# Up products of four FFNs from seven block products in place of eight, with the down part added chunk by chunk

## The chip, the cores and the metric

The kernel runs on one core of a Trainium2 chip. The metric is the device time of one execution in microseconds (us); the runs shown are of the same build.

## The reference

x has 512 tokens and 1024 features (D = 1024, F = 2816), all in float32. FFN 0 belongs to a first block with a recurrent mixer and a convolution; FFN 1 to 4 belong to a second block with a pooling mixer and an attention with shared keys and values:

```
FFN 0:       u = conv(rmsnorm(x) @ w_up); x = x + rmsnorm((silu(gate) * val) @ w_down)
FFN 1 to 4:  x = x + 0.5 * (silu(u @ wg) * (u @ wu)) @ wd      u = rmsnorm_2(x, gain)
order:       first mixer, FFN 0, FFN 1, pooling mixer, FFN 2, shared keys/values (kv),
             FFN 3, attention (dq, attn, w_o), FFN 4, final norm
```

## The kernel before

**Layout.** Activations lie feature-major: xT is 128 partitions by 8 k-tiles of 512 tokens. A norm isn't applied to x. Its gain goes into the operand (xghi, xglo), and its factor R (one value for each token) is multiplied onto the product.

**Exactness.** Each float32 product is made of three matmuls on rounded parts. ScalarE copies raw to whi (the rounded high part), VectorE subtracts to get wlo, and `three` accumulates wlo x xhi, whi x xlo and whi x xhi into one PSUM bank (L827, L828, L829).

**Units.** Weights come in units of 1024 x 256 (1 MB) through two slots. SP loads raw, ScalarE writes whi (L552), VectorE writes wlo (L1219); GpSimd takes some of these splits (L455). A unit of an up product has two output tiles of 128 features, each of 8 k-tiles x 3 matmuls of 512 columns. FFN 1 to 4 each have 11 pairs of a gate unit (slot 0) and a value unit (slot 1).

**Stages of an FFN.** `first_units` works through the first pair tile by tile as the operand arrives, a loop does the other ten pairs, and all 22 gated tiles are kept as ahi and alo. Then `project` makes the down product: two loop turns of two column blocks, each of k-splits 8, 8 and 6, with four PSUM banks (`ring`). Out of PSUM, VectorE adds 0.5 times the group to xT (L1423). It makes the next operand's low part (L1229) and ScalarE its high part (L572) and its square, which GpSimd sums (L470).

**Order.** Every engine has one queue in program order; what runs next to what is fixed by where each instruction stands and by semaphores. `sum_norm` is the matmul with ones that completes a norm. At FFN 1 the residual of FFN 0 is first completed by `add_normed` (L1436, L1442); at FFN 2 the pooling sums (L319, L1524, L1549) run on VectorE and GpSimd; FFN 3 follows the narrow kv product (`key_extras` adds two matmuls), FFN 4 the projection w_o.

## Time and profile before

| | |
|---|---|
| median of 3 runs | 2567.89 us (2566.75 to 2568.83) |
| profiled execution, first to last instruction | 2566.1 us |
| what lies around the span, median less span | 1.8 us |
| TensorE busy | 2471.6 us, 96% |
| VectorE busy | 1284.2 us, 50% |
| ScalarE busy | 797.1 us, 31% |
| GpSimd busy | 279.6 us, 11% |

The profile is of one execution, which has no device time of its own beside its span; so a difference in the span is carried over to the median. Engines: PE is TensorE's matmuls, PEld its weight loads, DVE VectorE, ACT ScalarE, POOL GpSimd, SP the engine that issues the loads. Line numbers are those of the kernel. A matmul's duration in the profile reaches over the start of the next, so that neighbouring starts give the rate.

### The profile page before, as it was taken

How to read it: one execution, taken by the hardware profiler on the slowest of the kernel's cores; microseconds unless marked ns; L12 is line 12 of the kernel's file. 1: busy time of each engine (PE TensorE's matmuls, PEld its weight loads, DVE VectorE, ACT ScalarE, POOL GpSimd, SP SyncE). 2: the span in 40 equal slices, each digit the busy share in tenths (PEclk: the TensorE clock that was granted, in tenths of full speed). 3: DMA queues.
4: the chain of work that ended last, by engine and by line, in shares of the span. 5: the costliest groups of instructions: out<-in, count | busy, mean ns of one | idle time of the engine just before them, and what ended most of it. 6: DMA issues, size and time to landing. Idle time of an engine off the chain costs nothing.

```text
span 2566.1 us, 28434 instructions
## 1 busy us (share of the span) xinstructions
PE 2471.6 (96%) x10762; PEld 1956.1 (76%) x10762; DVE 1284.2 (50%) x1429; ACT 797.1 (31%) x892; POOL 279.6 (11%) x128
## 2 busy tenths in 40 slices
PE   7999799999899999789999999999989999999998
PEld 5888677788688888568888778888856668788886
DVE  5687578762544433664443354443376743444423
ACT  4324443332332222232223232222233332222221
POOL 1211322211200000410000000000121201000000
PEclk9999999999999999899999999999999999999999
DMA  4221223322233222222322233322220113322321
GB/s 145 82 66 50 79 85 98 97 91 90 66 98 98 90 91 98 81 62 86 98 94 91 86 99 98 98 94 90 74 58 21 33 49 98 98 87 93 94 91 61
DMA packets 217220, 215.51 MB, mean 84 GB/s; under 512 B 10321, under 2 KB 214736, under 8 KB 217168
## 3 DMA queue, kind: packets, MB, share of 16 engines
q1 hardware_dynamic: 216624, 214.61, 26.4%
q8 instruction: 34, 0.56, 0.1%
q10 hardware_dynamic: 544, 0.20, 0.0%
q14 instruction: 18, 0.15, 0.0%
HBM read 212.70 MB, written 2.10 MB: 84 GB/s over the span
## 4 chain that ended last, share of the span: by engine, by line
PE 90%; DVE 7%; ACT 2%; issue 1%; DMA 0%; DVEq 0%; POOL 0%; ACTq 0%
PE bank L827 28%; PE bank L829 28%; PE bank L828 27%; PE bank L1192 1%; PE bank L1162 1%; DVE xglo L1229 1%; PE bank L1165 1%; PE bank L926 1%; DVE xT L1442 1%; DVE wlo L1219 1%; ACT xghi L572 1%; ACT whi L552 1%; DVE work L1463 0%; DVE PT L1699 0%; DVE Y L1436 0%
## 5 line engine op out<-in xcount | busy, mean ns | idle before, releaser
L827 PE MATMUL bank<-xghi,wlo 128*128 128x512 f32 x2064 | 827.3, 401 | 61.6 <-DVE xglo L1229 59.4
L828 PE MATMUL bank<-xglo,whi 128*128 128x512 f32 x2064 | 820.2, 397 | 0.0
L829 PE MATMUL bank<-xghi,whi 128*128 128x512 f32 x2064 | 819.9, 397 | 0.0
L1219 DVE TENSOR_TENSOR wlo<-raw,whi 128x2048 fp32r<-128x2048 f32 x185 | 426.6, 2306 | 583.2 <-ACT whi L552 583.1
L552 ACT ACTIVATE whi<-raw 128x2048 fp32r<-128x2048 f32 x210 | 400.1, 1905 | 536.0 <-PE bank L829 525.0
L827 PEld LDWEIGHTS bank<-xghi,wlo 128*128 128x128 f32 x2064 | 390.3, 189 | 169.2 <-DVE xglo L1229 56.4
L829 PEld LDWEIGHTS bank<-xghi,whi 128*128 128x128 f32 x2064 | 390.0, 189 | 96.0
L828 PEld LDWEIGHTS bank<-xglo,whi 128*128 128x128 f32 x2064 | 390.7, 189 | 95.1 <-issue 1.7
L827 PE MATMUL bank<-ahi,wlo 128*128 128x512 f32 x880 | 347.6, 395 | 0.0
L829 PE MATMUL bank<-ahi,whi 128*128 128x512 f32 x880 | 347.6, 395 | 0.0
L828 PE MATMUL bank<-alo,whi 128*128 128x512 f32 x880 | 347.6, 395 | 0.0
L722 ACT ACTIVATE ahi<-work 128x512 f32 (+1 forms) x110 | 68.8, 636 | 460.7 <-DVE work L1491 460.7
L827 PEld LDWEIGHTS bank<-ahi,wlo 128*128 128x128 f32 x880 | 164.9, 187 | 40.6 <-issue 0.2
L829 PEld LDWEIGHTS bank<-ahi,whi 128*128 128x128 f32 x880 | 164.9, 187 | 40.5
L828 PEld LDWEIGHTS bank<-alo,whi 128*128 128x128 f32 x880 | 164.9, 187 | 40.2
L1482 DVE TENSOR_TENSOR work<-bank,R 128x512 f32<-128x512 f32 x110 | 75.0, 690 | 208.6 <-PE bank L829 206.9
L710 ACT ACTIVATE work<-work 128x512 f32<-128x512 f32 x110 | 69.4, 632 | 300.2 <-DVE work L1471 276.9
L455 POOL TENSOR_TENSOR wlo<-raw,whi 128x2048 fp32r<-128x2048 f32 x25 | 121.3, 4850 | 352.8 <-ACT whi L552 352.8
L470 POOL TENSOR_TENSOR acc<-sq 128x512 f32<-128x512 f32 x11 | 16.1, 1465 | 1263.7 <-ACT sq L679 1230.8
L1471 DVE TENSOR_TENSOR work<-bank,R 128x512 f32<-128x512 f32 x110 | 74.3, 687 | 153.8 <-PE bank L829 148.7
L470 POOL TENSOR_TENSOR acc<-acc,sq 128x512 f32<-128x512 f32 x62 | 86.9, 1401 | 508.4 <-ACT sq L679 480.5
L1463 DVE SCALAR_TENSOR_TENSOR work<-work,cw 128x511 f32<-128x511 f32 x88 | 110.5, 1266 | 14.6 <-ACT work L703 4.5
(231 smaller groups left out, 1857.6 us busy)
## 6 DMA issues: line engine op xcount, KB each, us to landing
raw<-in_ffn_w_up_dram SPq DMA_DIRECT2D x22, 1024.0 KB, 5.1
raw<-in_ffn_pre_wg_dram SPq DMA_DIRECT2D x22, 1024.0 KB, 5.3
raw<-in_ffn_pre_wu_dram SPq DMA_DIRECT2D x22, 1024.0 KB, 5.4
raw<-in_ffn_post_wg_dram SPq DMA_DIRECT2D x22, 1024.0 KB, 5.3
raw<-in_ffn_post_wu_dram SPq DMA_DIRECT2D x22, 1024.0 KB, 5.3
raw<-in_ffn_pre_wd_dram SPq DMA_DIRECT2D x16, 1024.0 KB, 5.2
raw<-in_ffn_post_wd_dram SPq DMA_DIRECT2D x16, 1024.0 KB, 5.2
raw<-in_w_in_dram SPq DMA_DIRECT2D x14, 1024.0 KB, 5.0
```

Source lines behind the costliest of these rows:

```text
L455: nc.gpsimd.tensor_tensor(wlo[:, c], raw[:, c], whi[:, c].bitcast(F32), ALU.subtract).then_inc(wlo_ready[s], 2)
L470: nc.gpsimd.tensor_tensor(acc[:, :], a0, tile(sq, k % 2), ALU.add).then_inc(acc_added, 1)
L552: nc.scalar.activation(whi[:, s * UNIT:(s + 1) * UNIT], raw[:, s * UNIT:(s + 1) * UNIT], ACT.Copy).then_inc(whi_ready[s], 2)
L710: nc.scalar.activation(tile(Tt, f), tile(Tt, f), ACT.Silu).then_inc(silu_ready, 1)
L722: nc.scalar.activation(tile(ahi, i * 2 + f), tile(At, f), ACT.Copy).then_inc(ahi_ready, 1)
L827: nc.tensor.matmul(bank, wlo_, xhi, start=first, stop=False)
L828: nc.tensor.matmul(bank, whi_, xlo, start=False, stop=False)
L829: return nc.tensor.matmul(bank, whi_, xhi, start=False, stop=last)
L1219: nc.vector.tensor_tensor(wlo[:, c], raw[:, c], whi[:, c].bitcast(F32), ALU.subtract).then_inc(wlo_ready[s], 2)
L1463: nc.vector.scalar_tensor_tensor(dst[:, sh:T], u[:, 0:T - sh], tap_col(i, tap, half, f), dst[:, sh:T], ALU.mult, ALU.add).then_inc(signal, 1)
L1471: nc.vector.tensor_tensor(tile(Ut if conv else Tt, f), ring[f][:, :], R[:, :], ALU.mult).then_inc(evacuated, 1)
L1482: nc.vector.tensor_tensor(tile(Ut if conv else At, f), ring[2 + f][:, :], R[:, :], ALU.mult).then_inc(evacuated, 1)
```

## The change

FFN 1 to 4 only. The up product of a unit (1024 x 256 weights, 512 tokens) is treated as a 2 x 2 block product. The weights are split by k-tile parity and by output tile, the tokens into two halves, and the block product is formed by the Winograd form of Strassen's scheme: seven block products of 128 x 128 by 256 columns for each of four pairs of k-tiles. In full:

- **Weights.** GpSimd makes the four sums of weight blocks (`unit_sums`): three into `sums`, one written over a raw block. ScalarE and VectorE split raw (2048 wide, part 0) and the sums (1536 wide, part 1) into high and low parts (`fill_up`).
- **Tokens.** For each pair of k-tiles `halves_act` widens the tiles with their gain into At, `halves_vec` makes the three differences into Tt, and both write seven half-width operands, high and low (`Xhi`, `Xlo`).
- **Products.** `chain` runs one of the seven (m1 to m7) over four pairs of k-tiles, 12 matmuls of 256 columns. Some partial results are copied out of PSUM by ScalarE (`keep`) and added by VectorE at the end (`take_unit`).
- **First pair.** `first_pair` runs m1, m2 and m4 as token operands arrive; m5, m6, m3 and m7 follow for both units.
- **Chunks.** The 11 pairs go in chunks of 2, 3, 3 and 3. After each chunk, `down_chunk` multiplies its 4 or 6 tiles (`chi`, `clo`) by their rows of the down weights for all 8 output tiles in 8 banks, and `take_down` adds 0.5 times each to xT. The 22-tile ahi and alo aren't used there.
- **Around it.** FFN 0's result is in Y1 and Ut, loops of FFN 1 to 4 and of w_o are unrolled, two pooling and kv operands get their own low part, oThi and oTlo lie where Xhi and Xlo of two token pairs lie, and the interleaving at each FFN's start is rewritten.

```diff
+CHUNKS = [2, 3, 3, 3]
+PAIR0 = [0, 2, 5, 8]
+UNIT0 = [0, 8, 18, 28]
...
+            def ffn(m):
+                which, l = FFN_WEIGHTS[m]
+                gate, val = kp(A[f"ffn_{which}_wg_2"][l]), kp(A[f"ffn_{which}_wu_2"][l])
+                down = kp(A[f"ffn_{which}_wd_2"][l])
+                for c, pairs in enumerate(CHUNKS):
+                    kt = 2 * pairs
+                    for i in range(PAIR0[c], PAIR0[c] + pairs):
+                        load(up_no(m, i, 0), 0, [(slot(raw, 0), gate[:, :, i * UC:(i + 1) * UC])])
+                        load(up_no(m, i, 1), 1, [(slot(raw, 1), val[:, :, i * UC:(i + 1) * UC])])
+                    k0 = 2 * PAIR0[c]
+                    for b in range(4):
+                        load(down_no(m, c, b), b % 2, [(slot(raw, b % 2, kt),
+                                                        down[:, k0:k0 + kt, b * UC:(b + 1) * UC])])
...
+            def unit_sums(m, i, h):
+                n, base = up_no(m, i, h), adds_base(m, i)
+                u = slot(raw, h).rearrange("p (j d) c -> p j d c", d=2)
+                a11, a12 = u[:, :, 0, 0:P], u[:, :, 1, 0:P]
+                a21, a22 = u[:, :, 0, P:2 * P], u[:, :, 1, P:2 * P]
+                s1, s2, s4 = (sums[h][:, k * 512:(k + 1) * 512].rearrange("p (j c) -> p j c", c=P) for k in range(3))
+                pool.wait_ge(raw_ready[h], (n - h) * 8 + 16)
+                nc.gpsimd.tensor_tensor(s1, a21, a22, ALU.add).then_inc(adds_done[h], 1)
+                nc.gpsimd.tensor_tensor(a21, a11, a21, ALU.subtract).then_inc(adds_done[h], 1)
+                pool.wait_ge(adds_done[h], base + 1)
+                nc.gpsimd.tensor_tensor(s2, s1, a11, ALU.subtract).then_inc(adds_done[h], 1)
+                pool.wait_ge(adds_done[h], base + 3)
+                nc.gpsimd.tensor_tensor(s4, a12, s2, ALU.subtract).then_inc(adds_done[h], 1)
+            def ffn_sums(m, first):
+                for i in range(first, FT // 2):
+                    unit_sums(m, i, 0)
+                    unit_sums(m, i, 1)
...
-            sum_squares("post_ffn", last_splits("down0", len(DOWN)))
-            for name in ("pre0", "mix0"):
-                sum_squares(name)
-            pool.wait_ge(groups_done, GB["pool"])
+            sum_squares("post_ffn", [UB["down0"] + 7, None])
+            pool.wait_ge(groups_done, GB["down0"] + 8)
+            unit_sums(1, 0, 0)
+            unit_sums(1, 0, 1)
+            sum_squares("pre0")
+            ffn_sums(1, 1)
+            sum_squares("mix0")
...
+            def fill_up(m, i, h, part, signal, value):
+                n = up_no(m, i, h)
+                if part == 0:
+                    a.wait_ge(raw_ready[h], (n - h) * 8 + 16)
+                    a.wait_ge(adds_done[h], adds_base(m, i) + 2)
+                    a.wait_ge(signal, value)
+                    nc.scalar.activation(whi[:, h * UNIT:(h + 1) * UNIT], raw[:, h * UNIT:(h + 1) * UNIT],
+                                         ACT.Copy).then_inc(whi_ready[h], 2)
+                else:
+                    a.wait_ge(adds_done[h], adds_base(m, i) + 4)
+                    a.wait_ge(signal, value)
+                    nc.scalar.activation(sxhi[h][:, :], sums[h][:, :], ACT.Copy).then_inc(whi_ready[h], 2)
+            def fill_down(m, c, b):
+                n, s, w = down_no(m, c, b), b % 2, 2 * CHUNKS[c] * UC
+                a.wait_ge(raw_ready[s], (n - s) * 8 + 16)
+                a.wait_ge(m7_done, strassen_no(m, PAIR0[c] + CHUNKS[c] - 1, b // 2) + 1)
+                dst = sxhi[b // 2][:, 0:w] if s else whi[:, (b // 2) * UNIT:(b // 2) * UNIT + w]
+                nc.scalar.activation(dst, raw[:, s * UNIT:s * UNIT + w], ACT.Copy).then_inc(whi_ready[s], 4)
...
+            def halves_act(m, pos, signal=None, value=None):
+                j = PAIR_ORDER[m][pos]
+                hi, (gain, off) = Xhi[PAIR_SLOT[m][j]], FFN_GAIN[m]
+                n = 4 * (m - 1) + pos
+                a.wait_ge(halves_ready, n)
+                for d in range(2):
+                    nc.scalar.activation(tile(At, d), tile(xT, 2 * j + d), ACT.Copy,
+                                         scale=col(gain, 2 * j + d + off)).then_inc(wide_ready, 1)
+                if signal is not None:
+                    a.wait_ge(signal, value)
+                a.wait_ge(wide_ready, 2 * n + 2)
+                nc.scalar.activation(hi[:, 0:HT], At[:, 0:HT], ACT.Copy).then_inc(halves_hi, 1)
+                nc.scalar.activation(hi[:, HT:3 * HT], At[:, T:2 * T], ACT.Copy).then_inc(halves_hi, 1)
+                a.wait_ge(halves_added, 3 * n + 3)
+                nc.scalar.activation(hi[:, 3 * HT:7 * HT], Tt, ACT.Copy).then_inc(halves_hi, 1)
...
+                for c, pairs in enumerate(CHUNKS):
+                    for i in range(PAIR0[c], PAIR0[c] + pairs):
+                        for h in range(2):
+                            if i == 0:
+                                continue
+                            fill_next(m, i, h, 0)
+                            keep(m, i, h, "m1")
+                            fill_next(m, i, h, 1)
+                            keep(m, i, h, "m5")
+                            if h:
+                                gate_act(m, i)
+                            elif i > PAIR0[c]:
+                                pair_act(m, i - 1)
+                            keep(m, i, h, "u2")
+                            keep(m, i, h, "m4")
+                    fill_down(m, c, 2)
+                    pair_act(m, PAIR0[c] + pairs - 1)
+                    fill_down(m, c, 3)
+                    if c + 1 < len(CHUNKS):
+                        for part in range(2):
+                            fill_up(m, PAIR0[c + 1], 0, part, down_done, group_no(m, c, 4))
...
+            for part in range(2):
+                fill_up(1, 0, 0, part, groups_done, GB["down0"] + 8)
             root("post_ffn")
-            for k in range(DT):
-                xg_hi(resid_ready, DT + k + 1, xT, "ffn_pre_norm_2", k)
-                square("pre0", k, xT)
-            up(1, "pre0")
-            project("down1", DOWN, "mix0", "mix_norm_2")
+            for part in range(2):
+                fill_up(1, 0, 1, part, groups_done, GB["down0"] + 8)
+            for pos in range(4):
+                a.wait_ge(resid_ready, DT + 2 * pos + 2)
+                halves_act(1, pos)
+                square("pre0", 2 * pos, xT)
+                square("pre0", 2 * pos + 1, xT)
...
+                late = (groups_done, GB["w_o"] + 8) if b > 1 else ()
+                halves_act(4, b, *late)
...
+                out_, plain, at_, c = {
+                    "m1": (bank_y[h][:, 0:HT], True, (0, 0), 0), "m2": (bank_x[h][:, 0:HT], True, (1, 0), 1),
+                    "m4": (bank_d[h][:, 0:HT], True, (1, 1), 6), "m7": (bank_y[h][:, 0:HT], True, (0, 1), 4),
+                    "m5": (bank_x[h][:, HT:T], False, 0, 3), "m6": (bank_y[h][:, 0:HT], False, 1, 5),
+                    "m3": (bank_x[h][:, HT:T], False, 2, 2)}[kind]
...
+            def chained(m, i, h):
+                u = strassen_no(m, i, h)
+                pe.wait_ge(m1_kept, u + 1)
+                chain(m, i, h, "m6", m6_done)
+                if i:
+                    chain(m, i, h, "m4", m4_done)
+                pe.wait_ge(m5_kept, u + 1)
+                chain(m, i, h, "m3", m3_done)
+                pe.wait_ge(u2_kept, u + 1)
+                chain(m, i, h, "m7", m7_done)
+            def strassen_unit(m, i, h):
+                n, u = up_no(m, i, h), strassen_no(m, i, h)
+                pe.wait_ge(wlo_ready[h], split_count(n, h) - 2)
+                pe.wait_ge(out_taken, 2 * u - 2)
+                if i == PAIR0[CHUNK_OF[i]]:
+                    pe.wait_ge(down_taken, group_no(m, CHUNK_OF[i] - 1, 4 * h + 4))
+                chain(m, i, h, "m1", m1_done)
+                chain(m, i, h, "m2", None)
+                pe.wait_ge(wlo_ready[h], split_count(n, h))
+                chain(m, i, h, "m5", m5_done)
+                chained(m, i, h)
...
+                for pos, h in order:
+                    j = PAIR_ORDER[m][pos]
+                    if pos == 0:
+                        pe.wait_ge(wlo_ready[h], split_count(up_no(m, 0, h), h) - 2)
+                        if m > 1:
+                            pe.wait_ge(out_taken, 2 * strassen_no(m, 0, h) - 2)
+                    pe.wait_ge(halves_ready, 4 * (m - 1) + pos + 1)
+                    for kind, done in (("m1", m1_done), ("m2", None), ("m4", m4_done)):
+                        ins = part_product(m, h, kind, j, pos == 0, pos == 3)
+                        if pos == 3 and done is not None:
+                            ins.then_inc(done, 1)
+                if between:
+                    between()
+                for h in range(2):
+                    pe.wait_ge(wlo_ready[h], split_count(up_no(m, 0, h), h))
+                    chain(m, 0, h, "m5", m5_done)
+                    chained(m, 0, h)
...
+                for g in range(4):
+                    group(g, range(kt - 2))
+                for g in range(4):
+                    group(g, range(kt - 2, kt))
+                for g in range(4, 8):
+                    group(g, range(kt))
...
+            def take_unit(m, i, h):
+                u = strassen_no(m, i, h)
+                t = (Tt, At)[h]
+                v.wait_ge(m3_done, u + 1)
+                v.wait_ge(u2_kept, u + 1)
+                nc.vector.tensor_tensor(t[:, 0:T], bank_x[h][:, :], kept[h][:, 0:T], ALU.add).then_inc(out_taken, 1)
+                v.wait_ge(m7_done, u + 1)
+                v.wait_ge(m4_kept, u + 1)
+                nc.vector.tensor_tensor(halves(t[:, T:2 * T]), rep_halves(bank_y[h][:, 0:HT]),
+                                        halves(kept[h][:, T:2 * T]), ALU.add).then_inc(out_taken, 1)
+                v.wait_ge(out_taken, 2 * u + 2)
...
+            def halves_vec(m, pos):
+                j = PAIR_ORDER[m][pos]
+                s, n = PAIR_SLOT[m][j], 4 * (m - 1) + pos
+                hi, lo = Xhi[s], Xlo[s]
+                v.wait_ge(wide_ready, 2 * n + 2)
+                nc.vector.tensor_tensor(halves(Tt[:, 0:T]), At.rearrange("p (o c) -> p o c", o=4)[:, 1::2, :],
+                                        halves(At[:, 0:T]), ALU.subtract).then_inc(halves_added, 1)
+                v.wait_ge(halves_added, 3 * n + 1)
+                nc.vector.tensor_tensor(Tt[:, T:T + HT], At[:, T + HT:2 * T], Tt[:, 0:HT], ALU.subtract
+                                        ).then_inc(halves_added, 1)
+                v.wait_ge(halves_added, 3 * n + 2)
+                nc.vector.tensor_tensor(Tt[:, T + HT:2 * T], At[:, T:T + HT], Tt[:, T:T + HT], ALU.subtract
+                                        ).then_inc(halves_added, 1)
+                v.wait_ge(halves_hi, 3 * n + 2)
+                nc.vector.tensor_tensor(lo[:, 0:HT], At[:, 0:HT], hi[:, 0:HT].bitcast(F32), ALU.subtract)
+                nc.vector.tensor_tensor(lo[:, HT:3 * HT], At[:, T:2 * T], hi[:, HT:3 * HT].bitcast(F32), ALU.subtract)
+                v.wait_ge(halves_hi, 3 * n + 3)
+                nc.vector.tensor_tensor(lo[:, 3 * HT:7 * HT], Tt, hi[:, 3 * HT:7 * HT].bitcast(F32), ALU.subtract
+                                        ).then_inc(halves_ready, 1)
...
+                for c, pairs in enumerate(CHUNKS):
+                    for i in range(PAIR0[c], PAIR0[c] + pairs):
+                        if i > PAIR0[c]:
+                            gate_pair(m, i - 1)
+                        if i:
+                            fill_next(m, i, 0, 0)
+                            fill_next(m, i, 0, 1)
+                        if i > PAIR0[c]:
+                            split_pair(m, i - 1)
+                        scale_gate(m, i)
+                        fill_next(m, i, 1, 0)
+                        fill_next(m, i, 1, 1)
+                        scale_silu(m, i)
+                    gate_pair(m, PAIR0[c] + pairs - 1)
+                    fill_down(m, c, 2)
+                    split_pair(m, PAIR0[c] + pairs - 1)
+                    fill_down(m, c, 3)
+                    if c + 1 < len(CHUNKS):
+                        for g in range(4):
+                            take_down(m, c, g)
...
+            for h in range(2):
+                for part in range(2):
+                    fill_up(1, 0, h, part)
             rstd("post_ffn")
-            add_normed(Y1, "post_ffn_g", DT, "up1", "ffn_pre_norm_2")
-            up(1, "pre0")
-            project("down1", DOWN, xT, 0.5, "pool", "mix_norm_2")
+            def scale_y(k):
+                nc.vector.scalar_tensor_tensor(ytile(k), ytile(k), col("post_ffn_g", k), R[:, :],
+                                               ALU.mult, ALU.mult).then_inc(resid_part, 1)
+            def add_y(k):
+                v.wait_ge(resid_part, DT + k + 1)
+                nc.vector.tensor_tensor(tile(xT, k), tile(xT, k), ytile(k), ALU.add).then_inc(resid_ready, 1)
+            def add_two(k):
+                scale_y(k)
+                scale_y(k + 1)
+                add_y(k)
+                add_y(k + 1)
+            add_two(0)
+            for pos in range(4):
+                if pos < 3:
+                    add_two(2 * pos + 2)
+                halves_vec(1, pos)
+            ffn(1, "pre0", plain_tail("pool", "mix_norm_2"))
```

## Rows read from the trace of the kernel before

**Rows 1.** The page's busy times: engine, us, share, instructions.

```profile
PE 2471.6 (96%) x10762; PEld 1956.1 (76%) x10762; DVE 1284.2 (50%) x1429; ACT 797.1 (31%) x892; POOL 279.6 (11%) x128
```

**Rows 2.** Stretches: from:to, length, busy us by engine, granted clock, DMA.

```profile
core 0: us, PE busy (x) PEld busy (x) DVE busy (x) ACT busy (x) POOL busy (x), PEclk, DMA share, GB/s
668.00:708.00 40.00, 27.95 (x101) 20.15 (x100) 30.24 (x28) 18.58 (x25) 13.78 (x8) 0.87 0.11 35
708.00:1056.00 348.00, 348.00 (x1493) 279.57 (x1492) 138.17 (x131) 95.64 (x91) 8.27 (x6) 1.00 0.29 91
1056.00:1121.00 65.00, 40.46 (x147) 30.37 (x146) 55.83 (x48) 23.53 (x29) 37.83 (x18) 0.82 0.21 66
1469.00:1509.00 40.00, 37.62 (x150) 28.68 (x149) 22.91 (x25) 18.65 (x21) 1.50 (x1) 0.96 0.48 145
1509.00:1857.00 348.00, 348.00 (x1493) 279.57 (x1492) 137.50 (x131) 94.97 (x89) 8.26 (x6) 1.00 0.28 87
2177.00:2200.00 23.00, 23.00 (x99) 18.17 (x98) 8.58 (x8) 8.69 (x9) 1.48 (x1) 1.00 0.31 92
```

**Rows 3.** Timeline, TensorE in FFN 1's up stage, first and thirteenth of 13.

```profile
899.75 0.40 PE L827 MATMUL bank<-xghi,wlo 128*128 128x512 f32 x1
...
902.55 0.40 PE L827 MATMUL bank<-xghi,wlo 128*128 128x512 f32 x1
```

**Rows 4.** Timeline, TensorE in w_in's token-major part, first and last of 97.

```profile
199.76 0.28 PE L829 MATMUL bank<-whi,xghi 128*128 128x256 f32 x1
...
211.12 0.28 PE L829 MATMUL bank<-whi,xghi 128*128 128x256 f32 x1
```

**Rows 5.** Groups by line and shape: count, busy us, mean ns, idle before.

```profile
L1219 DVE TENSOR_TENSOR wlo<-raw,whi 128x2048 fp32r<-128x2048 f32 x185 | 426.6, 2306 | 583.2 <-ACT whi L552 583.1
L552 ACT ACTIVATE whi<-raw 128x2048 fp32r<-128x2048 f32 x210 | 400.1, 1905 | 536.0 <-PE bank L829 525.0 <-DMA raw<-in_w_in_dram 10.5 <-DMA raw<-in_w_uq_dram 0.5
...
L829 PEld LDWEIGHTS bank<-xghi,whi 128*128 128x128 f32 x2064 | 390.0, 189 | 96.0
...
L1482 DVE TENSOR_TENSOR work<-bank,R 128x512 f32<-128x512 f32 x110 | 75.0, 690 | 208.6 <-PE bank L829 206.9
...
L1283 DVE TENSOR_TENSOR SC<-V,fkb 128x1024 f32<-128x1024 f32 x7 | 8.5, 1218 | 0.0
...
L805 ACT ACTIVATE PT<-bank 128x512 f32<-128x512 f32 x4 | 2.4, 597 | 0.3
```

**Rows 6.** One line's instructions on GpSimd: duration ns, min/median/max.

```profile
L470 POOL TENSOR_TENSOR acc<-acc,sq x62: 1285/1332/2286, 19.0 to 2544.8; 128x512 f32<-128x512 f32 x62
...
L489 POOL TENSOR_TENSOR V<-fkb x7: 1894/2131/3947, 79.3 to 170.6; 128x1024 f32<-128x1024 f32 x7
...
L319 POOL TENSOR_TENSOR PW<-PW x5: 1895/2225/2979, 1068.2 to 1087.1; 128x1024 f32<-128x1024 f32 x5
```

**Rows 7.** DMA issues: KB each, median us to landing.

```profile
raw<-in_ffn_pre_wg_dram SPq DMA_DIRECT2D x22, 1024.0 KB, 5.3
```

**Rows 8.** Timeline, VectorE beside GpSimd: start, us.

```profile
678.96 0.68 DVE L1442 TENSOR_TENSOR xT<-xT,Y 128x512 f32<-128x512 f32 x1
...
681.07 1.27 POOL L470 TENSOR_TENSOR acc<-sq 128x512 f32<-128x512 f32 x1 [4.85 <-ACT sq L567]
681.11 1.79 DVE L1442 TENSOR_TENSOR xT<-xT,Y 128x512 f32<-128x512 f32 x1
...
1075.91 4.96 POOL L455 TENSOR_TENSOR wlo<-raw,whi 128x2048 fp32r<-128x2048 f32 x1
...
1076.42 2.47 DVE L1524 TENSOR_TENSOR PU<-bank,R 128x512 f32<-128x512 f32 x4
```

**Rows 9.** Timeline, VectorE where the four entries begin or end.

```profile
668.33 0.69 DVE L1421 COPY Y<-bank 128x512 f32 x1 [3.51 <-PE bank L829]
672.85 3.92 DVE L1436 SCALAR_TENSOR_TENSOR Y<-Y,cols,R 128x512 f32<-128x512 f32 x1 [3.82 <-ACT R L589]
...
1108.14 3.43 DVE L1229 SCALAR_TENSOR_TENSOR xglo<-xT,cols,xghi 128x512 fp32r<-128x512 f32 x2
...
1482.65 5.38 DVE L1229 SCALAR_TENSOR_TENSOR xglo<-xT,cols,xghi 128x512 fp32r<-128x512 f32 x8
...
2177.21 0.69 DVE L1423 SCALAR_TENSOR_TENSOR xT<-bank,xT 128x512 f32 x1 [4.91 <-PE bank L829]
```

518 lines of the change are left out of this document (392 added, 126 removed), and 3 rows, old and new, of the table PHASES.

## Prediction

> **What bounds the kernel now.** I read four views in turn. First the busy shares: TensorE is busy 96% of the span [rows 1]. Then stretches cut where one stage hands over to the next: in FFN 1 to 4, TensorE is busy for 348.0 us of 348, at full clock, once the first gate and value units are through (two of the four stretches are shown); it is short of work only in the stretches between the end of one stage and the end of the next FFN's first pair (40, 65, 40 and 23 us long, the first two at a mean clock of 0.87 and 0.82) [rows 2]. So a matmul saved behind the first pair is saved time as long as the other engines keep up; work added to the entry stretches is on the path. Third, the beat: a matmul's duration overlaps its neighbours, so starts count. Twelve 512-column starts take 2.80 us, 0.2333 us each [rows 3]; ninety-six 256-column starts in the token-major part of w_in take 11.36 us, 0.1183 us each, with one weight load per matmul as in the change [rows 4]. Fourth, who shares what with GpSimd.
>
> **Up products.** A pair (gate and value unit) goes from 96 matmuls of 512 columns, 22.40 us, to 2 x 7 x 4 x 3 = 168 of 256, 19.88 us: 2.52 us less, not an eighth, since two half-width matmuls cost 1.4% more than one. The first pair of each FFN belongs to the entry; ten follow: 4 x 10 x 2.52 = **101 us less**. Down keeps its 528 matmuls of 512 columns. The load of 128x128 weights has a mean of 189 ns, longer than 118, but it is overlapped: [rows 4] is itself a stream with such loads. One unit is 9.94 us, one of its seven chains 1.42 us.
>
> **What the other engines must do in 9.94 us.** VectorE [rows 5]: two adds out of PSUM at 0.65; a split of 128x2048 at 2.29; one of 128x1536, estimated 1.76 from 2.29 and 1.22; two products or splits of 128x1024 at 1.22. Sum 7.8 us. ScalarE: copies of 2048 (1.90) and 1536 (estimate 1.5), one of 1024 (estimate 1.06), four keeps of 256 out of PSUM (estimate 0.4 from 0.60 for 512): 6.1 us. GpSimd: four sums of 128x512 at about 1.3 [rows 6], 5.2 us. A 128x1024 sum of two separate blocks has the minimum of a contiguous one, 1895 against 1894 ns, so I give the strided slices no surcharge. Each engine alone fits. Every load lands some 5.3 us after its issue [rows 7].
>
> **GpSimd and VectorE don't overlap.** An xT add takes VectorE 0.68 us alone and 1.79 when a GpSimd sum of 1.27 us started 0.04 before it. VectorE's takes out of PSUM ran four in 2.47 us beside a GpSimd split [rows 8]. So a VectorE instruction with two SBUF inputs and a GpSimd sum take turns; one out of PSUM doesn't. The Trainium skill has that rule (SBUF — State Buffer, "Who interferes with whom"): the pair of ports is an exclusive lock for a whole instruction, and a VectorE instruction with two SBUF inputs contends with a GpSimd one that reads SBUF. By that rule, the trace agrees, my sum is the one below; with three engines that never met it would be 2534 (no stalls, entries at their lower bound). Of VectorE's 7.8 us, 6.5 have two SBUF inputs; with the sums that is 11.7 us in a unit of 9.94.
>
> **Stalls inside the chunks.** Only some units meet sums: the last units of a chunk are followed by down loads, which have none, and the next chunk's first sums fall under down. In a three-pair chunk number the units 0 to 5. Raw for unit 3 lands 1.9 us into unit 1, for unit 4 some 5.3 into unit 2, for unit 5 some 5.7 into unit 3. Walking the queues, each sum alternating with a VectorE instruction, VectorE enters unit 2 late by 2.0 us, unit 3 by 2.5, unit 4 by 2.9. TensorE can bear that: a unit's splits, done at 5.2 and 6.9 without sums, are wanted at 9.9 and 12.8, and the keep behind a gate scaled at 2.9 is wanted at 8.5. What reaches it is ScalarE's order. In unit 3 its second copy (for unit 4) waits for unit 4's fourth sum, done at 6.3, and the keep of the fifth product is queued behind it: 7.9 + 0.4 = 8.3, where TensorE's third product wants that bank's half at 7.1. That is 1.3 us, and 1.7 in unit 4. I take 3 us for a chunk of three pairs, nothing for the one of two: 3 x 3 x 4 = **36 us more**. Bounds: 0, if the queues fall more kindly (both stalls hang on under 2 us), and 60 (5 a chunk) if sums come at 1.5.
>
> **The entries.** These are the largest doubt. The old first pair leaves 5.6 us of matmuls after its last tile; the new one has 18 (2.1 us), the sum over squares (0.9), and eight chains (11.4): 14.4. Making one pair of k-tiles ready costs VectorE 4.2 us with its waits (0.69, two of about 0.42, then splits of 256, 512 and 1024) instead of 2 x 0.75, and ScalarE's two widening copies (1.5) don't overlap it, since At is reused.
> FFN 1: the sums can't start before down0 ends (668.3). Slot 0's take 5.2, to 673.5; then VectorE's four splits (8.1) and slot 1's sums (5.2) alternate: 686.8. Only now comes the residual, which starts at 672.85 today [rows 9]. Two scaled adds 2.9; a first turn of 7.1; two of 9.5 (a next double add 2.9, halves 4.2, two sums of squares 2.4); a last of about 7: near 721; plus 14.4, 736 against 708: 28 us.
> FFN 2: last xglo ends at 1111.6 [rows 9]. VectorE's splits grow from 2.3 to 8.1, tiles from 6.0 to 16.8, ScalarE's copies show three times (4.5), sums add some 3, less 2 that the xglo wait for GpSimd today: 1135; plus 14.4, 1149 against 1121: 28.
> FFN 3: VectorE is free for it at 1482.7 [rows 9], splits 8.1, tiles 16.8, copies 4.5: 1512; seven or so of the next units' sums on the way at 1.2: 1520.5; plus 14.4, 1535 against 1509: 26.
> FFN 4: the last two stores reuse oThi, so ScalarE waits for w_o's end at 2177.0 with the takes of the last two tiles behind it on VectorE; those end near 2182 (today 2177.9 [rows 9]), the last pair of tiles near 2188, slot 1's first split near 2191; then 54 half matmuls 6.4, 0.9 and 11.4: 2211 against 2200: 12 with the waits.
> Sum **94 us more**. Bounds: 67 if no sum of GpSimd meets VectorE there (17, 22, 18, 10), 115 if sums come at 1.45 and TensorE begins the last 14.4 us at 1.2 GHz; the mean clocks of 0.87 and 0.82 in [rows 2] say that it spends part of such a stretch there, after standing idle.
>
> **Other edits.** The take into xT goes from 8 to 32 a FFN (0.69 each, out of PSUM and under down's matmuls; if not covered, 17 us a FFN). Down's first four groups leave their last two tiles for later, 11.2 us (5.6 in the first chunk) against the last pair's split at about 5.9: at most 0.5. SP's queue has its loads unrolled and in the same order behind the same two slots, with 16 down loads for 12, inside a DMA share of 0.29 [rows 2]. No term for them.
>
> **Sum.** 2566.1 - 101 + 36 + 94 = 2595. The runs' median lies 1.8 over this execution's span: **2597 us**.
>
> **The rivals.**
> 1. Faster. The gain of 101 stands and GpSimd's sums fall into VectorE's idle time (it is idle whenever it waits for a unit's last chain). For: sums are short, and the two queues need not alternate as strictly as I walk them. Against: in the entries VectorE is never idle. It decides as soon as entries and stalls together cost under 101. Entries 67, stalls 10: 2544.
> 2. The port as bound. If a strided sum takes what a 128x1024 one takes, 1.9, a unit needs 14.1 us of turns and the backlog reaches every chunk: about 8 us a chunk, 96 in all, with entries at 115: 2678. For: no row has a slice of four blocks. Against: two blocks cost nothing.
> 3. The products don't keep the 118 ns over thousands of unrolled matmuls (their loads or instruction supply): 10 ns more would be 7392 x 0.01 = 74 us. [Rows 4] speak against it: 22 us without a gap. 2670.
>
> **Chances.** My forecast's case (2565 to 2640, slower nearly throughout) 0.55; rival 1 0.31; rival 2 0.09; rival 3 0.05. A difference under 0.2%, 5 us, can't be told from none: 0.08, taken from the seam between the first two. Faster 0.32, same 0.08, slower 0.60. The range goes from 2566.1 - 101 + 67 + 1.8 = 2534 to 2566.1 - 101 + 115 + 60 + 1.8 = 2642. The forecast's own range is 2573 to 2640.
>
> **What would show it.** 256-column starts every 0.118 us, and 9.94 us a unit away from stalls, show the gain; if so, entry stretches of about 68, 93, 66 and 35 us in place of 40, 65, 40 and 23 carry the loss. Idle TensorE in the fourth and fifth unit of a chunk behind ScalarE's keep, itself behind GpSimd's sum, shows the stalls. GpSimd sums much longer than 1.3 us would be rival 2. Entries under 80 us in sum with idle TensorE under 10 us elsewhere would make me wrong in sign.

## The result, and the profile after

The changed kernel takes 2555.61 us (median of 4 runs) against 2567.32 for the kernel before (4 runs): ratio 0.9948, 95% interval 0.9936 to 0.996, so 0.5% faster. The forecast was 2597 and slower (0.60 against 0.32 for faster); it was wrong in sign. The time lies in the whole range of 2534 to 2642, but below the forecast's own 2573 to 2640. The span went from 2566.1 to 2554.0 us. The executions of one kernel lie up to 8 us apart (2550.28 to 2555.92 here, 2540.43 to 2548.36 in experiment 5), which bears on every difference of a few us below, and one of the eleven of experiment 3 fell in a slow state (2853.59 us).

The page's busy times, to be held against [rows 1]:

```profile
PE 2371.9 (93%) x13930; PEld 2056.2 (81%) x13930; DVE 1768.5 (69%) x1695; ACT 1048.8 (41%) x1308; POOL 948.3 (37%) x478
```

TensorE lost 100 us of busy time, but the span only 12. Stretches of the changed kernel, with the columns of [rows 2]; the first two are FFN 1's entry (end of the stage before to the end of the first pair) and the rest of FFN 1, the third one up stretch of three pairs, then the entries of FFN 2, 3 and 4:

```profile
667.50:733.50 66.00, 31.02 (x175) 27.61 (x174) 45.84 (x50) 35.45 (x49) 35.28 (x23) 0.66 0.10 32
733.50:1053.40 319.90, 319.90 (x2211) 297.47 (x2210) 240.27 (x179) 143.39 (x171) 153.59 (x78) 1.00 0.32 99
775.40:834.90 59.50, 59.50 (x505) 59.45 (x504) 53.33 (x34) 32.05 (x41) 41.17 (x17) 1.00 0.36 114
1053.40:1146.30 92.90, 40.96 (x222) 35.38 (x221) 72.83 (x68) 37.78 (x51) 54.55 (x34) 0.69 0.15 46
1466.10:1535.90 69.80, 42.38 (x223) 36.52 (x222) 47.69 (x44) 33.30 (x43) 30.33 (x18) 0.73 0.21 68
2175.70:2215.20 39.50, 25.94 (x171) 24.83 (x171) 22.61 (x19) 18.86 (x26) 13.46 (x10) 0.78 0.12 39
```

The reader is to see two things. Behind the first pair TensorE is busy for 319.90 us of 319.90 at full clock: there is no stall in any chunk but one of 0.16 us (below). In the entries it is busy for 26 to 42 us of 40 to 93, at a mean clock of 0.66 to 0.78, where [rows 2] had 0.82 to 1.00.

The ledger of the spans, each stretch cut at TensorE's starts in the same way in both kernels:

| | before | after | difference |
|---|---|---|---|
| entries of FFN 1 to 4 | 40.6, 65.7, 40.5, 23.3 | 66.0, 92.9, 69.8, 39.5 | +98.1 |
| ten further pairs, 4 times | 224.0 each | 198.4 each | -102.4 |
| down, 4 times | 123.2 each | 121.5 each | -6.8 |
| all the rest | | | -1.0 |
| sum | | | -12.1 |

The beat, first and last start of the 504 matmuls of that three-pair stretch, against [rows 4]:

```profile
775.44 0.28 PE L1100 MATMUL bank<-Xhi,wlo 128*128 128x256 f32 x1
...
834.85 0.28 PE L1102 MATMUL bank<-Xhi,whi 128*128 128x256 f32 x1
```

59.41 us for 503 steps is 0.1181 each, and a pair is 19.8 us.

GpSimd and VectorE in the middle of that stretch. Units of this chunk begin at 775.4, 785.4, 795.3, 805.2, 815.1 and 825.0. Timeline, GpSimd, then VectorE, then ScalarE (start, us):

```profile
798.54 3.34 POOL L579 TENSOR_TENSOR sums<-raw 128x512 f32<-128x512 f32 x1
801.84 2.81 POOL L580 TENSOR_TENSOR raw<-raw 128x512 f32<-128x512 f32 x1
804.61 2.28 POOL L582 TENSOR_TENSOR sums<-sums,raw 128x512 f32<-128x512 f32 x1
806.97 2.37 POOL L584 TENSOR_TENSOR sums<-raw,sums 128x512 f32<-128x512 f32 x1
809.30 3.34 POOL L579 TENSOR_TENSOR sums<-raw 128x512 f32<-128x512 f32 x1
...
817.74 2.36 POOL L584 TENSOR_TENSOR sums<-raw,sums 128x512 f32<-128x512 f32 x1
```

```profile
800.66 2.84 DVE L1909 TENSOR_TENSOR sxlo<-sums,sxhi 128x1536 fp32r<-128x1536 f32 x1
...
818.87 3.38 DVE L1906 TENSOR_TENSOR wlo<-raw,whi 128x2048 fp32r<-128x2048 f32 x1
822.18 1.75 DVE L1909 TENSOR_TENSOR sxlo<-sums,sxhi 128x1536 fp32r<-128x1536 f32 x1
```

```profile
820.19 1.49 ACT L877 ACTIVATE sxhi<-sums 128x1536 fp32r<-128x1536 f32 x1 [2.41 <-issue]
821.58 0.36 ACT L908 ACTIVATE kept<-bank 128x256 f32<-128x256 f32 x1
```

The turns are there as forecast: a split of 128x2048 that takes 2.29 us alone takes 3.38 when it has to let one sum pass, and a sum that takes 1.27 alone ends some 1.15 us after the VectorE instruction that it met (the split from 800.66 ends at 803.50, the sum from 801.84 at 804.65). GpSimd, never idle here, needs 10.76 us for a unit's sums (798.54 to 809.30), 0.84 more than the unit's 9.92. So it falls behind, but by less than a microsecond a unit, and the chunk ends first. In the fifth unit, which begins at 815.1, the keep of the fifth product ends at 821.94, 6.8 us into the unit; TensorE wants it at 7.1. Over the twelve three-pair chunks this keep ends 6.6 us into the fifth unit in seven, 6.8 to 6.9 in four and 7.1 in one, the first of FFN 3. There TensorE does wait, and the stretch takes 59.7 us in place of 59.5:

```profile
1624.26 0.36 ACT L908 ACTIVATE kept<-bank 128x256 f32<-128x256 f32 x1
...
1624.49 0.28 PE L1102 MATMUL bank<-Xhi,whi 128*128 128x256 f32 x1
1624.68 0.38 PE L1100 MATMUL bank<-Xhi,sxlo 128*128 128x256 f32 x1
```

So the margin was 0 to 0.5 us.

### The profile page after: what moved, and what is told of

Its sections match the earlier page's. It is cut to its first block, busy times and chain, and to the rows that moved or that the text cites. A ratio compares the mean times of both kernels' runs of the same rounds, so it can differ in the third digit from the quotient of the medians.

```text
span 2554.0 us, 34670 instructions
## 1 busy us (share of the span) xinstructions
PE 2371.9 (93%) x13930; PEld 2056.2 (81%) x13930; DVE 1768.5 (69%) x1695; ACT 1048.8 (41%) x1308; POOL 948.3 (37%) x478
## 4 chain that ended last, share of the span: by engine, by line
PE 86%; DVE 8%; ACT 3%; issue 1%; POOL 1%; DMA 0%; DVEq 0%; ACTq 0%; POOLq 0%
PE bank L1106 15%; PE bank L1107 15%; PE bank L1108 15%; PE bank L1100 11%; PE bank L1102 11%; PE bank L1101 11%; PE bank L1583 2%; PE bank L1553 1%; PE bank L1556 1%; PE bank L1205 1%; DVE Xlo L1994 1%; DVE xglo L1621 1%; DVE work L1982 1%; DVE wlo L1906 1%; DVE work L1853 0%
## 5 line engine op out<-in xcount | busy, mean ns | idle before, releaser
L1100 PE MATMUL bank<-Xhi,wlo 128*128 128x256 f32 x1408 | 405.8, 288 | 126.6 <-DVE Xlo L1994 98.6
L1102 PE MATMUL bank<-Xhi,whi 128*128 128x256 f32 x1408 | 404.6, 287 | 0.0
L1101 PE MATMUL bank<-Xlo,whi 128*128 128x256 f32 x1408 | 403.4, 287 | 0.0
L579 POOL TENSOR_TENSOR sums<-raw 128x512 f32<-128x512 f32 x88 | 175.3, 1992 | 576.7 <-DMA raw<-in_ffn_pre_wg_dram 239.9
L1100 PE MATMUL bank<-Xhi,sxlo 128*128 128x256 f32 x1056 | 300.8, 285 | 0.0
L1101 PE MATMUL bank<-Xlo,sxhi 128*128 128x256 f32 x1056 | 298.4, 283 | 0.0
L1102 PE MATMUL bank<-Xhi,sxhi 128*128 128x256 f32 x1056 | 298.2, 282 | 0.0
L1106 PE MATMUL bank<-xghi,wlo 128*128 128x512 f32 x656 | 264.8, 404 | 23.2 <-DVE xglo L1621 21.3
L1102 PEld LDWEIGHTS bank<-Xhi,whi 128*128 128x128 f32 x1408 | 275.4, 196 | 0.0
L1108 PE MATMUL bank<-xghi,whi 128*128 128x512 f32 x656 | 260.7, 397 | 0.0
L1107 PE MATMUL bank<-xglo,whi 128*128 128x512 f32 x608 | 241.8, 398 | 0.0
```

Source lines behind the costliest of these rows:

```text
L579: nc.gpsimd.tensor_tensor(s1, a21, a22, ALU.add).then_inc(adds_done[h], 1)
L1100: nc.tensor.matmul(bank, wl, x, start=first, stop=False, skip_group_check=True)
L1101: nc.tensor.matmul(bank, w, xl, start=False, stop=False, skip_group_check=True)
L1102: return nc.tensor.matmul(bank, w, x, start=False, stop=last, skip_group_check=True)
L1106: nc.tensor.matmul(bank, wlo_, xhi, start=first, stop=False)
L1107: nc.tensor.matmul(bank, whi_, xlo, start=False, stop=False)
```

## The experiments

All are edits of the changed kernel, each timed beside the kernel before. "After" is the changed kernel's 2555.6. An entry is best read in two parts, cut where VectorE has the last pair of x tiles ready (the end of its last split, L1994 in the changed kernel): the front, which VectorE, ScalarE and GpSimd make, and the tail, TensorE's last 18 matmuls, the sum over squares and the eight chains. Front + tail in us, from the timeline of each run:

| | FFN 1 | FFN 2 | FFN 3 | FFN 4 |
|---|---|---|---|---|
| changed kernel | 48.9 + 17.0 | 74.9 + 18.0 | 50.6 + 19.2 | 15.0 + 24.5 |
| 5, sums held back | 48.9 + 15.9 | 74.8 + 17.0 | 43.9 + 16.3 | 11.3 + 25.2 |
| 6, FFN 1's order | 46.3 + 17.5 | 74.9 + 17.8 | 50.8 + 19.0 | 15.0 + 24.4 |
| 7, second buffer | 48.6 + 18.2 | 74.2 + 16.9 | 48.9 + 16.3 | 15.0 + 24.5 |
| 8, TensorE kept busy | 49.0 + 15.9 | 74.8 + 15.9 | 50.6 + 16.3 | 15.1 + 24.4 |
| 9, down's weights swapped | 49.0 + 17.0 | 74.8 + 18.0 | 50.9 + 16.3 | 15.0 + 24.4 |
| 10, together | 46.3 + 17.4 | 74.2 + 15.9 | 41.2 + 19.3 | 11.3 + 24.7 |

Fronts that an edit doesn't touch agree within 0.3 us. Tails don't: experiment 9 touches no entry, and its tail in FFN 3 is 2.9 us shorter, at a granted clock of 1.00 in place of 0.84:

```profile
1516.70:1535.90 19.20, 18.47 (x118) 16.67 (x119) 9.59 (x11) 9.24 (x14) 0.00 (x0) 0.84 0.00 1
1516.90:1533.20 16.30, 15.59 (x118) 14.43 (x119) 9.56 (x11) 9.14 (x14) 0.00 (x0) 1.00 0.00 1
```

(FFN 3's tail in the changed kernel, then in experiment 9.) So a gain of up to 3 us in a tail of one execution can't be put down to an edit.

**1. A fifth sum in every unit.**

```diff
+                nc.gpsimd.tensor_tensor(s4, a21, a22, ALU.add)
                 nc.gpsimd.tensor_tensor(s1, a21, a22, ALU.add).then_inc(adds_done[h], 1)
```

> Each unit's sums on GpSimd are preceded by a fifth one (128x512, its result is overwritten), so VectorE meets one more turn of about 1.1 us in every unit. Theory A, the stalls inside a chunk were absent by a margin of half a microsecond: in the fifth unit of a chunk ScalarE's keep of the fifth product ended 6.6 us into the unit and TensorE wants it at 7.1. Then a chunk of three pairs loses 2 to 3 us, twelve chunks 24 to 36, the entries some 10 for the turns they meet: span 2588 to 2600 against 2554.0 of the changed kernel. Theory B, the double slots swallow lateness as a whole: only the entries pay, 2562 to 2566, and TensorE stays without a gap in the chunks.

Measured: 2601.68 us, ratio 1.0137 (1.012 to 1.0153), 46 over after. The three-pair stretches grow from 59.5 to 64.1, 62.6 and 62.5 us, the entries from 268.2 to 273.1 in sum. The trace shows the stall. TensorE, around one stall of the middle stretch, and the keep that ended it:

```profile
813.25 0.28 PE L1103 MATMUL bank<-Xhi,sxhi 128*128 128x256 f32 x1
815.03 0.39 PE L1101 MATMUL bank<-Xhi,sxlo 128*128 128x256 f32 x1 [1.50 <-ACT sq L909]
```

```profile
812.80 1.91 ACT L873 ACTIVATE whi<-raw 128x2048 fp32r<-128x2048 f32 x1 [5.16 <-POOL raw L581]
814.61 0.37 ACT L909 ACTIVATE sq<-bank 128x256 f32<-128x256 f32 x1
```

The total is as expected, but partly by luck: the twelve stretches lost 41.7 us (24 to 36 expected), the entries 4.9 (10 expected). And the place is another: TensorE goes from the fifth product (sxhi) to the sixth and waits for the keep of the first, behind ScalarE's first copy, which waits for the second counted sum (L581). GpSimd's unit is now 11.78 us long (L579 at 804.26 and at 816.04), and everything runs at its pace: neither it nor VectorE has a gap from 804 to 827, and TensorE's units are 11.78 long too (815.03 to 826.81).

**2. The same, with the keep of the fifth product ahead of the second copy.**

```diff
                             keep(m, i, h, "m1")
-                            fill_next(m, i, h, 1)
                             keep(m, i, h, "m5")
+                            fill_next(m, i, h, 1)
```

> The kernel with a fifth GpSimd sum a unit (2601.7, entries 273.0 us in sum, the nine three-pair stretches beyond the first unit some 3 to 4.5 us longer each), with one change: ScalarE keeps the fifth product ahead of its second copy. Theory A: what reached TensorE was the keep queued behind the copy that waits for the last sum; the three-pair up stretches go back to 59.5 to 60 us and only the entries keep their 5 us: 2558 to 2566. Rival B: with five sums the turns between GpSimd and VectorE use up the unit itself, and the stall moves to the wait for the splits: 2585 to 2602.

Measured: 2602.44 us, 1.0139 (1.0124 to 1.0155). Theory A fell: nothing came back. The edit moved the keep of the fifth product, and TensorE waited in both runs for the keep of the first, behind the first copy. The outcome is rival B's, the wait isn't: it stays where it was in 1. A unit still takes 11.78 us and neither GpSimd nor VectorE has a gap, so with five sums I take their turns as the bound; that no other order of ScalarE's queue helps is argued from this, not tried.

**3. A fifth sum only in the last value unit of each three-pair chunk,** after the two sums that the first copy waits for:

```diff
+                if h and i in (4, 7, 10):
+                    nc.gpsimd.tensor_tensor(s4, a12, a22, ALU.add)
                 nc.gpsimd.tensor_tensor(s2, s1, a11, ALU.subtract).then_inc(adds_done[h], 1)
```

> Changed kernel (2555.6), with a fifth GpSimd sum only in the last value unit of each three-pair chunk, between its second and third sums, so that ScalarE's first copy of that unit is not held up but its second one is. Theory A: in the changed kernel the keep of the fifth product, queued behind that second copy, ends 6.9 us into its unit where TensorE wants it at 7.1, so one more turn (1.1 to 2.2 us) stalls TensorE 0.9 to 2.0 us, twelve times: 2566 to 2580. Rival B: only GpSimd's own rate over many units can reach TensorE, and one more sum a chunk vanishes in the down part: 2554 to 2558.

Measured: 2563.2 us, 0.9984 (0.9975 to 0.9994), 7.6 over after; the three-pair stretches are 60.2 to 60.5 us, and 60.7 in FFN 3's first. This time the stall is where the forecast had put it:

```profile
821.43 0.28 PE L1104 MATMUL bank<-Xhi,whi 128*128 128x256 f32 x1
822.38 0.39 PE L1102 MATMUL bank<-Xhi,sxlo 128*128 128x256 f32 x1 [0.67 <-ACT kept L910]
```

```profile
820.57 1.49 ACT L879 ACTIVATE sxhi<-sums 128x1536 fp32r<-128x1536 f32 x1 [3.46 <-issue]
821.96 0.37 ACT L910 ACTIVATE kept<-bank 128x256 f32<-128x256 f32 x1
```

The third product (sxlo behind the fourth's whi) waits for the keep of the fifth. The gap is 0.95 less the beat of 0.12, 0.83 us: the fourth sum ends 1.05 us later in its unit than in the changed kernel, one turn, less the margin of 0.3. There are twelve such gaps, one in each three-pair chunk, and the stretches are 9.6 us longer in sum; in this execution the entries are 2.7 shorter, in their tails. Theory A holds in place, but the time lies below its 2566 (and above B's 2558): it allowed for up to two turns and it was one.

**4. The same, with that keep ahead of the second copy** (the edit of 2).

> The kernel before this one (a fifth sum in the last value unit of a three-pair chunk), with ScalarE's keep of the fifth product ahead of its second copy. Theory A: the order of ScalarE's queue is what carries the late sum to TensorE here; with it gone the splits behind the copy are wanted only some 3 us later and the stall goes: 2553 to 2559. Rival B: the stall moves to another wait, as with five sums in every unit: 2564 or more.

Measured: 2560.97 us, 0.9975 (0.9965 to 0.9986); stretches 60.1 us (60.4 in one), so 0.6 of stall in place of 0.7 to 0.9. The gap ahead of the third product is gone, and the next one shows:

```profile
825.34 0.28 PE L1104 MATMUL bank<-Xhi,sxhi 128*128 128x256 f32 x1
825.97 0.39 PE L1102 MATMUL bank<-Xhi,wlo 128*128 128x256 f32 x1 [0.35 <-ACT kept L910]
```

That is the seventh product, waiting for the keep that still stands behind the copy. So both theories hold in part, and the time lies between their ranges: the order of ScalarE's queue carries the late sum, and moving one keep only hands the wait to the next.

**5. Sums of the second and later pairs held back until the entry's tiles are done** (FFN 1 to 4):

```diff
                 for i in range(first, FT // 2):
+                    if i == 1:
+                        pool.wait_ge(halves_ready, 4 * m)
```

> GpSimd starts the sums of the second pair of each FFN only when all four token operands are ready; nothing else changes. Theory A, in the entries VectorE is the path and each GpSimd sum that it meets costs it a turn of 1.1 us: eight such sums stand in FFN 3's entry and four in FFN 4's, so 10 to 13 us less, span 2541 to 2544. Rival B, the turns fall beside the path: 2554 within 1. Rival C, the sums then come late for the second pair (8 sums of 1.3 us against about 8 us until ScalarE wants the first two): up to 5 us more at each of FFN 3 and 4.

Measured: 2543.32 us, 0.9911 (0.9895 to 0.9928), 12.3 under after in the median and 15.4 in the span (2538.6). The entries are 64.9, 91.9, 60.2 and 36.5 us: 14.7 less in sum, of which 9.6 in FFN 3 and 3.0 in FFN 4, and the chunks still have no stall (319.9), so rival C's did not come. Only the fronts show the turns: 6.7 less in FFN 3 and 3.8 in FFN 4. The 1.1, 1.0 and 2.9 in FFN 1 to 3 are shorter tails, and in FFN 1 and 2 the front is unchanged to 0.1 us. FFN 3's second weight slot and tile on VectorE, in the changed kernel and then in this one:

```profile
1491.46 3.17 DVE L1906 TENSOR_TENSOR wlo<-raw,whi 128x2048 fp32r<-128x2048 f32 x1 [0.64 <-ACT whi L872]
1494.55 2.81 DVE L1909 TENSOR_TENSOR sxlo<-sums,sxhi 128x1536 fp32r<-128x1536 f32 x1
1497.29 1.75 DVE L1982 TENSOR_TENSOR work<-work 128x512 f32<-128x512 f32 x1
1499.07 1.37 DVE L1985 TENSOR_TENSOR work<-work 128x256 f32<-128x256 f32 x1
```

```profile
1489.76 2.29 DVE L1908 TENSOR_TENSOR wlo<-raw,whi 128x2048 fp32r<-128x2048 f32 x1 [0.65 <-ACT whi L874]
1491.96 1.75 DVE L1911 TENSOR_TENSOR sxlo<-sums,sxhi 128x1536 fp32r<-128x1536 f32 x1
1493.63 0.69 DVE L1984 TENSOR_TENSOR work<-work 128x512 f32<-128x512 f32 x1
1494.35 0.42 DVE L1987 TENSOR_TENSOR work<-work 128x256 f32<-128x256 f32 x1
```

Each sum that meets VectorE costs it 0.9 to 1.1 us, on an instruction of 0.42 as on one of 2.29.

**6. A new order in FFN 1's entry:** the residual first, one of the four weight splits behind each token pair.

```diff
-            for h in range(2):
-                for part in range(2):
-                    fill_up(1, 0, h, part)
             rstd("post_ffn")
...
                 halves_vec(1, pos)
+                h, part = ((0, 0), (1, 0), (0, 1), (1, 1))[pos]
+                fill_up(1, 0, h, part)
```

> At FFN 1 ScalarE takes the root first and VectorE begins with the residual; the four weight splits of the first pair stand behind one token pair each. Theory A, the old order left VectorE idle from 668 to 672 and 678 to 681 and put 13 us of splits ahead of the residual, all on the path: 6 to 8 us less, span about 2547, FFN 1's entry 59 us in place of 66. Rival B, the entry is held by the sum of all VectorE's work and turns wherever the splits stand, which only moves the idle time: within 2 us of 2554.

Measured: 2553.14 us, 0.9942 (0.9926 to 0.9959). FFN 1's entry goes from 66.0 to 63.7, other entries don't move. Of VectorE's 7.3 us idle in front 4.0 are filled (3.3 are left until R is there), but the residual now meets the second slot's sums and the splits meet the sums of squares: VectorE is busy for 51.6 us in the entry in place of 45.8. Rival B comes nearest, with 2.2 us in the span where it allowed 2.

**7. A second buffer for every second widened token pair** (FFN 1 to 3).

```diff
-                a.wait_ge(halves_ready, n)
+                At = wide(m, pos)
+                a.wait_ge(halves_ready, n - 1 if pos and m < 4 else n)
```

> Changed kernel, but in FFN 1 to 3 every second pair of tiles is widened into a second buffer, so that ScalarE's two widening copies (0.75 each) run while VectorE splits the pair before. Theory A: those copies stand open three times an entry in FFN 2 and FFN 3, as the forecast counted (4.5 us each); in FFN 1 the residual adds cover them: FFN 2 and 3 shorter by 4.5 each, near 2547. Rival B: VectorE is held up by turns with GpSimd and by the ends of its own steps, not by the copies: each entry shorter by less than 1 us, 2553 to 2556.

Measured: 2549.09 us, 0.9927 (0.9913 to 0.994). FFN 3's entry is 4.6 us shorter, as if as counted, FFN 2's 1.8 and FFN 1's none (+0.8). But the copies can only shorten a front, and the fronts are 1.7, 0.7 and 0.3 shorter; 2.9 and 1.1 are in the tails. So the match with 4.5 is luck, and theory A's 4.5 a time wasn't there. The span is 4.8 us shorter.

**8. TensorE kept busy in its waits.**

```diff
+                    for _ in range(WARM[m].get((pos, h), 0)):
+                        x = PAIR_SLOT[m][PAIR_ORDER[m][0]]
+                        nc.tensor.matmul(banks[7][:, 0:HT], slot(whi, 0)[:, 0, 0:P], Xhi[x][:, 0:HT],
+                                         start=True, stop=True)
                     pe.wait_ge(halves_ready, 4 * (m - 1) + pos + 1)
```

> Changed kernel, but while TensorE waits for the next pair of x tiles in an entry it runs extra matmuls of 256 columns into an unused bank (14, 20 and 24 ahead of tiles 2, 3 and 4 in FFN 1; 10, 20, 28 in FFN 2; 10 and 18 ahead of tiles 3 and 4 in FFN 3; 34 ahead of tile 2 in FFN 4), each batch sized to end about when the tile comes. Theory A: TensorE begins the last tile of an entry at 1.2 GHz because it stood idle; kept busy it takes the last 18 matmuls in 2.1 us in place of 3.3 to 4.0 and the eight chains in 11.4 in place of 12.7 to 13.0: entries shorter by 3 us in FFN 1 to 3 and by 1 in FFN 4, about 10 in all, near 2546. Rival B: the batches are too short to change the granted clock, or end late: 2554 to 2560.

Measured: 2550.11 us, 0.9935 (0.9921 to 0.9948), 5.5 under after, about half of what was expected. The entries are 1.1, 2.2, 2.9 and 0.0 us shorter. The entries of FFN 1 to 3:

```profile
667.80:732.70 64.90, 33.86 (x233) 30.92 (x232) 46.01 (x50) 35.48 (x49) 35.23 (x23) 0.79 0.10 33
1052.60:1143.30 90.70, 46.00 (x279) 40.76 (x278) 73.88 (x67) 37.79 (x51) 55.44 (x34) 0.74 0.15 47
1463.20:1530.10 66.90, 40.62 (x251) 35.57 (x250) 47.62 (x44) 33.20 (x43) 30.56 (x18) 0.82 0.23 71
```

More matmuls (233 for 175 in FFN 1), a higher granted clock (0.79 for 0.66), and a shorter stretch, with the fronts unchanged. The last 18 matmuls take 2.1 to 2.6 us in place of 3.3 to 4.0, as expected. The eight chains don't come down from 12.7 to 13.0 to 11.4; they take 12.7 at full clock. FFN 1's in the changed kernel and here:

```profile
720.70:733.50 12.80, 12.16 (x98) 11.72 (x97) 6.91 (x5) 8.58 (x12) 9.36 (x7) 0.99 0.01 1
720.00:732.70 12.70, 12.06 (x98) 11.62 (x97) 7.07 (x5) 8.58 (x12) 10.30 (x8) 1.00 0.00 0
...
731.20 0.38 PE L1102 MATMUL bank<-Xhi,wlo 128*128 128x256 f32 x1 [0.64 <-ACT sq L910]
```

Their 1.3 us over the beat aren't the clock's, and a wait of 0.64 for ScalarE's keep is part of them: this is the half that didn't come. The half that came isn't the edit's for sure. All five executions have a mean clock of 0.969 to 0.971, against 0.961 to 0.966 in the changed kernel's four, but tails of 15.9 in FFN 1 and 16.3 in FFN 3 also stand in runs without extra matmuls (experiments 5, 7 and 9); only FFN 2's 15.9 stands in no run but this one and 10.

**9. Down's weights swapped:** even column blocks in sxhi and sxlo, odd ones in whi and wlo.

```diff
-                        if s:
+                        if not s:
                             left, left_lo = sxhi[b // 2][:, at_], sxlo[b // 2][:, at_]
```

> The even down blocks are split into the sums' buffers (sxhi, sxlo) and the odd ones into whi and wlo, the other way round than in the change. In the changed kernel down matmuls start every 0.227 us from the sums' buffers and every 0.233 us from whi. Theory A, the place of the weights in SBUF makes the difference: then the even blocks become the fast ones and the mean of the down stretches stays 0.230, span 2554 within 1. Rival B, the block's turn or PSUM banks make it: the odd blocks stay the fast ones.

Measured: 2557.75 us, 0.996 (0.9946 to 0.9974), 2.1 over after in the median and 3.5 under it in the span (2550.5, with the short tail in FFN 3): no difference from after. It was made to place the 6.8 us that down gave and nobody forecast. In the changed kernel down's starts are 0.2333 us apart with weights in whi and wlo (even blocks, as before) and 0.2267 in sxhi and sxlo (odd blocks); swapped, they are 0.2333 in whi and wlo (now odd) and 0.2269 in sxhi and sxlo (now even), each a mean over 1008 steps. So it goes with the buffer, not with the block. The rows of one line in the changed kernel (count, duration in ns min/median/max) show the same:

```profile
L1107 PE MATMUL bank<-clo,whi x352: 393/395/397, 753.6 to 2526.4; 128*128 128x512 f32 x176
L1107 PE MATMUL bank<-clo,sxhi x352: 389/389/389, 756.4 to 2534.6; 128*128 128x512 f32 x176
```

Half of 528 matmuls at 0.0067 less is 1.77 us a FFN, against 1.7 found. Why one buffer is quicker to multiply from stays open.

**10. The edits of 5, 6, 7 and 8 together.**

> Changed kernel with the four edits that helped by themselves: the sums of later pairs held back until the entry's tiles are done (-15.4), the new order in FFN 1 (-2.2), a second widening buffer (-6.5) and TensorE kept busy in its waits (-5.5). If they add up: 2526. They overlap in FFN 3, where the held-back sums and the second buffer shorten the same steps, so 2524 to 2534.

Measured: 2536.87 us, 0.988 (0.9865 to 0.9895): the fastest, 18.7 under after and 1.2% under the kernel before, and 3 over the expected 2524 to 2534. The entries are 63.6, 90.1, 60.5 and 36.0 us, 250.2 in sum. (In FFN 1 ScalarE's copies for the second slot stand ahead of the squares here, behind them in 6.) The fronts add up: they are 16.5 us shorter in sum, where 5, 6 and 7 gave 10.5, 2.6 and 2.8 by themselves. The tails don't: only FFN 2's is shorter. In FFN 3 the last pair is ready 2.7 us sooner than with the held-back sums alone, yet the entry is no shorter (60.5 against 60.2), because the extra matmuls, sized for tiles that came later, are now in the way:

```profile
1499.90 1.34 PE L1399 MATMUL bank<-Xhi,whi 128*128 128x256 f32 x10
...
1503.20 2.28 PE L1399 MATMUL bank<-Xhi,whi 128*128 128x256 f32 x18
```

The last pair is ready at 1502.2, and its first matmul starts at 1505.32, behind them. Without the two batches it could have started some 3 us sooner (an estimate from these rows; no run has it).

## Why the prediction was wrong

**The step that failed: stalls inside the chunks, 36 us more.** It measured nothing but 0.16 us: 319.9 us of 319.9 in all four FFNs. The mechanism was right and the place was right, the size was not. The walk had VectorE late by 2.0, 2.5 and 2.9 us on entering units 2, 3 and 4; its first takes come 0.8, 1.7 and 2.5 us behind the unburdened pace (the takes at 794.89, 805.66 and 816.42 against 784.16 in steps of 9.92). The second copy of unit 3 started 4.2 us into the unit (809.43), not at 6.3, and its keep ended at 6.0, not 8.3. In unit 4, where 8.8 was forecast (1.7 too late), it ended at 6.8.

Where the two microseconds went can be followed along the walk's own chain. It had raw for unit 4 landing 5.3 us into unit 2 and the fourth sum done at 6.3 in unit 3: 10.9 us for four sums. Measured, the first of the four starts at 798.54, 3.3 into unit 2, and they take 10.8. So 2.0 of the 2.2 us were there before the first sum, and only the rest is in the sums. They were there because the load left early. It waits for VectorE's second split in unit 1:

```profile
787.66 2.29 DVE L1906 TENSOR_TENSOR wlo<-raw,whi 128x2048 fp32r<-128x2048 f32 x1
789.87 2.86 DVE L1909 TENSOR_TENSOR sxlo<-sums,sxhi 128x1536 fp32r<-128x1536 f32 x1
...
792.77 0.37 SPq L434 DMA_DIRECT2D raw<-in_ffn_pre_wg_dram  x1
```

That is 7.4 us into unit 1. A landing at 5.3 less the 5.3 of a load puts it at 9.9 in the walk: 6.9 for the splits without sums, and 3.0 of turns. The trace has 6.1 and 1.2 (0.15 on the product at 786.29, none on the first split, 1.1 on the second). In the next chunk, where the sums of unit 3 start 1.8 us into unit 1 as walked (1.9), the splits meet two turns, the load leaves at 8.2 and the sums of unit 4 start at 3.6. So fewer turns met those splits, they cost less each, and their start was put too late; how the walk came to its 3.0 is not on record, and how the rest divides stays open.

The price of a turn is one part that can be measured. The forecast gave each sum its whole duration, about 1.3 us. What a sum takes from VectorE is 1.09 (3.38 against 2.29), and [rows 8] held that number: 1.79 against 0.68 is 1.11. A unit's turns are 6.5 plus 4 x 1.09, 10.9 us, close to the measured 10.76; the forecast had 11.7. From the start of unit 3's sums GpSimd has no gap, so 0.2 us more a sum would have put the fourth sum of unit 4 up to 1.7 us later (eight sums), and the stalls would have come: this is argued from the trace, since no run changes the price. Experiments 1 and 3 change the number of sums and show how near the edge is: one more in every unit costs 46 us, one more in three units of each FFN 7.6. So the 36 wasn't a wild number, but a threshold that the kernel keeps by 0 to 0.5 us and the walk overstepped by 1.3 and 1.7. Without this term the sum would have been 2561, and faster.

**Up products, -101.** Measured -102.4. The beat of 0.118 from [rows 4] held over the 6720 unrolled matmuls behind the first pairs, so rival 3 was not there.

**Entries, +94.** Measured +98.1: 25.4, 27.2, 29.3 and 16.2 against 28, 28, 26 and 12. The nearness is in part luck, since larger errors cancel. The tail was put at 14.4 and took 17.0, 18.0 and 19.2 us in FFN 1 to 3: even at full clock it is 15.9 (the eight chains take 1.3 more than their beat, which no term held), and the rest goes with the clock (0.84 to 0.90 granted in these tails). The fronts of FFN 1, 2 and 3 were 4, 4 and 1 us shorter than walked. (The terms given for FFN 1 add up to 722.8, not 721.) FFN 1's walk in steps: the first slot's sums end at 672.8 (forecast 673.5), the four splits at 685.2 (686.8), the last tile at 716.5 (721), the entry at 733.5 (736). FFN 4 was short by 4.2: its last tiles meet four sums of the next pair, which no term held (experiment 5 gets 3.0 back). Of the copies counted at 4.5 in FFN 2 and 3, the fronts of experiment 7 give back 1.7 in FFN 3 and 0.7 in FFN 2. The clock was a bound and not a term; the short tails of experiment 8 are 6.2 us less over four entries. The 27 us between lower bound and value, put down to sums meeting VectorE and to waits, is explained to a good third: 10.5 goes from the fronts when the later pairs' sums are held back, and no run here moves the first pairs' own sums.

**Other edits, 0.** Right but for down's beat, -6.8, which no row of before could show, since no down product there used these buffers. The -1.0 left is in no stretch of its own.

**The sum.** Stalls -36, down -6.8, up -1.4, entries +4 and the rest -1.0 make 41 us under the forecast span of 2595. The largest, the stalls, turned the sign.

**The rivals.** Rival 1 happened in its outcome, by its stated condition (entries and stalls together under 101, measured 98), but not by its reason: the entries stayed at 98, not 67, and within the chunks GpSimd's sums didn't fall into idle time, since the units in the middle of a chunk have none (VectorE's instructions follow without a gap from 797.6 to 829.2). The forecast's own sign of being wrong, entries under 80, was too strict: with no stalls anything under 101 was enough. Rival 2, the shared port as the bound, is real one sum further on (experiments 1 and 2). Its condition, strided sums that take 1.9 alone, was not met: 1.27 alone (the minimum of the four lines is 1.26 to 1.27). The rule of the Trainium skill ("SBUF — State Buffer", section "Who interferes with whom"), an exclusive lock, is borne out by the rows of GpSimd and VectorE above in that they take turns; the trace adds the price, 1.09 us for a sum that takes 1.27 alone, so some 0.2 of a sum keeps nobody waiting.

## What to carry to other kernels

Price a turn at the shared port by what it adds to the partner's instruction (here 1.09 us for a 128x512 sum), not by the duration of the intruder, and ask for the period of the loop in turns against the period of the bound: 10.76 against 9.92 over three units is harmless (0.16 us in twelve chunks), 11.8 is not. A term that exists only beyond a threshold is to be forecast as a chance and not as a mean: here 0 or 36 hung on under 2 us in the walk. When a change saves matmuls, look for what it adds in front of the first one: four entries took back 98 of 109 us, and 18 of them came back in experiment 10, most of it by holding the later pairs' sums back. And cut a stretch where its limit changes before putting a gain down to an edit: the whole of FFN 3's entry said 4.6 us for the second buffer, its front 1.7.

## What the runs showed of the hardware

- The port changes hands instruction by instruction: a GpSimd sum of 1.27 us lasts up to 3.4 beside VectorE, and costs VectorE 0.9 to 1.1 us whether its instruction takes 0.42 or 2.29 alone.
- 512-column matmuls started every 0.2267 us with weights in one pair of buffers and every 0.2333 in another; swapping the buffers moved it along.
- The same last part of FFN 3's entry took 16.3 us at a granted clock of 1.00 and 19.2 at 0.84, in executions whose kernels don't differ there (experiment 9 and the changed kernel).
- Extra matmuls in TensorE's waits came with a granted clock of 0.79 for 0.66 in FFN 1's entry, which was 1.1 us shorter; in experiment 10, with tiles that came sooner, they held TensorE up by some 3 us in FFN 3.
